# Stores of the gated values moved to GpSimd's queue, a half-tile wait, and another pass order for the third tile, in a two-layer decoder kernel

## The reference

```python
def swiglu(x, w_gate_up, w_down):
    gu = x @ w_gate_up
    g, u = jnp.split(gu, 2, axis=-1)
    return (jax.nn.silu(g) * u) @ w_down
```

## Time and profile before

| | |
|---|---|
| median of the runs | 1989.75 us (1989.35 to 1995.39, 3 runs) |
| profiled execution | 1989.12 us, its span 1987.1 us |
| granted clock of TensorE | 0.999 |
| TensorE busy | 1968.9 us, 99% of the span |
| VectorE busy | 1317.0 us, 66% |
| ScalarE busy | 921.7 us, 46% |
| GpSimd busy | 1208.8 us, 61% |
| DMA | 414.99 MB, mean 209 GB/s |

### The profile page before, as it was taken

One profiled execution on the slowest core, in us unless ns is written; L12 is line 12 of the kernel. 1 busy time (PEld: TensorE's weight loads), 2 busy tenths in 40 slices (PEclk: granted clock), 3 DMA queues, 4 the chain that ended last, 5 costly groups with the idle time before them and its releaser, 6 DMA issues.

```text
span 1987.1 us, 28787 instructions
## 1 busy us (share of the span) xinstructions
PE 1968.9 (99%) x9979; PEld 1654.7 (83%) x9979; DVE 1317.0 (66%) x1749; ACT 921.7 (46%) x1930; POOL 1208.8 (61%) x1055
## 2 busy tenths in 40 slices
PE   9999999999999999999999999999999999999998
PEld 8898988888888888888888788788888888887886
DVE  6765452688777877564675677779766676645567
ACT  7434333366544555432345465456554544432233
POOL 5343222657988898656664112474988888846566
PEclk9999999999999999999999999999999999999999
DMA  7574545835767878795853123553667667687683
GB/s 219 181 238 170 172 158 210 309 119 170 257 229 261 255 242 255 245 402 168 273 181 75 43 93 100 187 184 121 226 219 250 230 222 258 210 340 264 220 266 129
DMA packets 292628, 414.99 MB, mean 209 GB/s; under 512 B 38129, under 2 KB 215305, under 8 KB 292497
## 3 DMA queue, kind: packets, MB, share of 16 engines
q1 hardware_dynamic: 257792, 307.61, 47.3%
q10 hardware_dynamic: 33280, 100.94, 14.0%
q0 software_dynamic: 1424, 4.77, 0.7%
HBM read 259.09 MB, written 154.17 MB: 208 GB/s over the span
## 4 chain that ended last, share of the span: by engine, by line
PE 95%; DMA 2%; DVE 1%; ACT 1%; issue 0%; POOL 0%; SPq 0%; POOLq 0%; DVEq 0%; ACTq 0%
PE ps L2552 22%; PE ps L2554 22%; PE ps L2553 22%; PE ps L2463 9%; PE ps L2465 5%; DMA scratch_hidden<-hidden 1%; PE ps L2928 1%; PE ps L2772 1%; PE ps L2773 1%; PE ps L2769 1%; PE ps L2607 1%; PE ps L2902 1%; PE ps L2571 1%; PE ps L2573 1%; PE ps L2572 1%; PE ps L2813 1%
## 5 line engine op out<-in xcount | busy, mean ns | idle before, releaser
L2552 PE MATMUL ps<-forms,mats 128*128 128x512 f32 x2016 | 787.1, 390 | 4.4 <-DVE X L1893 3.0
L2554 PE MATMUL ps<-forms,mats 128*128 128x512 f32 x2016 | 784.6, 389 | 0.0
L2553 PE MATMUL ps<-forms,mats 128*128 128x512 f32 x2016 | 784.5, 389 | 0.0
L1097 POOL TENSOR_TENSOR mats<-sum_a,mats 128x256 fp32r<-128x256 f32 (+2 forms) x384 | 407.3, 1066 | 347.5 <-ACT mats L1349 346.6
L2552 PEld LDWEIGHTS ps<-forms,mats 128*128 128x128 f32 x2016 | 378.5, 188 | 86.1 <-issue 7.6
L2554 PEld LDWEIGHTS ps<-forms,mats 128*128 128x128 f32 x2016 | 378.5, 188 | 78.6
L2553 PEld LDWEIGHTS ps<-forms,mats 128*128 128x128 f32 x2016 | 378.6, 188 | 77.2
L1893 DVE TENSOR_TENSOR X<-ps,X 128x512 f32<-128x512 f32 x390 | 268.0, 690 | 191.6 <-PE ps L2554 186.1
L1349 ACT ACTIVATE mats<-sum_a 128x256 fp32r<-128x256 f32 (+2 forms) x392 | 201.3, 516 | 316.8 <-PE ps L2554 295.7
L1870 DVE TENSOR_TENSOR mats<-stream_raw,mats 128x256 fp32r<-128x256 f32 (+2 forms) x302 | 279.9, 929 | 21.3 <-ACT mats L1349 20.8
L1349 ACT ACTIVATE mats<-stream_raw 128x256 fp32r<-128x256 f32 (+2 forms) x302 | 156.4, 519 | 241.1 <-PE ps L2554 241.0
(11 more groups left out here) (271 smaller groups left out, 2621.1 us busy)
## 6 DMA issues: line engine op xcount, KB each, us to landing
forms<-scratch_forms ACTq DMA_DIRECT2D x182, 512.0 KB, 5.7
scratch_forms<-prep_forms SPq DMA_DIRECT2D x161, 512.0 KB, 3.3
stream_raw<-in_w_gate_up_dram SPq DMA_DIRECT2D x88, 512.0 KB, 5.5
scratch_forms<-head_forms SPq DMA_DIRECT2D x49, 512.0 KB, 3.2
scratch_hidden<-hidden SPq DMA_DIRECT2D x84, 256.0 KB, 5.3
prep_raw<-in_w_down_dram SPq DMA_DIRECT2D x38, 512.0 KB, 5.2
stream_raw<-scratch_hidden SPq DMA_DIRECT2D x32, 512.0 KB, 4.8
forms<-scratch_forms SPq DMA_DIRECT2D x28, 512.0 KB, 6.0
```

Of the source, the lines that this page charges most:

```text
L1097: pool.tensor_tensor(blocks(m[:, q, 1, :], it.width), stream_source(it, q), blocks(m[:, q, 0, :].bitcast(F32), it.width), ALU.subtract).th ...
L2552: mm(dst, ah, bh, start=OPENS[q] and k == 0, stop=False, skip_group_check=True)
L2553: mm(dst, ah, bl, start=False, stop=False, skip_group_check=True)
L2554: m = mm(dst, al, bh, start=False, stop=k == w - 1, skip_group_check=True)
```

## The change

Three parts.

First, the third tile (t = 2) of the value and gate stage is no longer `v_gate_tile(2)`, which takes the three passes interleaved for each of eight blocks k. Its high-by-high and high-by-low passes come first, for all k, waiting for ScalarE's high parts and the PSUM bank that is written; the low-by-high pass follows and waits for VectorE.

Second, in the plain item product j = 2 waits for the first half of the last tile's evacuation alone.

Third, `store_hidden` moves from SyncE's queue to GpSimd's. SyncE had issued the 22 pairs of a layer at i = 9, then between its other transfers at q = 1 and q = 3 of i = 10 to 27, and at 28, 29 and 31. GpSimd issues all 22 pairs, at q = 1 of i = 9 to 30, each for the item before. Its waits for `u_dve` (that VectorE has written the tile) and the transfers themselves are unchanged.

```diff
@@ SyncE @@
-            def store_hidden(it, halves=range(2)):
-                l, k = it.layer, up_no[it.n]
-                for e in halves:
-                    sp.wait_ge(u_dve, 5 * k + 4 + e)
-                    sp.dma_start(scr_h[l][:, :, it.tile, e, :].rearrange("g p n -> p g n"),
-                                 hidden_of(it)[e][:].rearrange("p (g n) -> p g n", g=4)).then_inc(hid_st[e], 16)
...
-                    if i in (9, 28, 29):
-                        store_hidden(its[i - 1])
-                    if i == 31:
-                        store_hidden(its[29])
...
                             if 10 <= i <= 27 and q in (0, 2):
                                 load_stream(its[i + 2], (q // 2,))
-                            if 10 <= i <= 27 and q in (1, 3):
-                                store_hidden(its[i - 1], (q // 2,))
@@ GpSimd @@
+            def store_hidden(it):
+                l, k = it.layer, up_no[it.n]
+                for e in range(2):
+                    pool.wait_ge(u_dve, 5 * k + 4 + e)
+                    pool.dma_start(scr_h[l][:, :, it.tile, e, :].rearrange("g p n -> p g n"),
+                                   hidden_of(it)[e][:].rearrange("p (g n) -> p g n", g=4)).then_inc(hid_st[e], 16)
...
                     for q in range(NQ):
+                        if 9 <= i <= 30 and q == 1:
+                            store_hidden(its[i - 1])
@@ TensorE, plain_item @@
                     if j == 2:
-                        pe.wait_ge(xt_ready, evac_before[norm] + 16)
+                        pe.wait_ge(xt_ready, evac_before[norm] + 15)
@@ TensorE, value and gate stage @@
-            for t in range(2, TT):
+            pe.wait_ge(xt_hi_ready, 6)
+            pe.wait_ge(bank_free[6], Kv[0][6])
+            for k in range(KT):
+                v_gate_pass(2, "hh", (k,), first=True)
+                v_gate_pass(2, "hl", (k,))
+            pe.wait_ge(bank_free[0], Kn[0] + 2)
+            pe.wait_ge(bank_free[1], Kn[1] + 2)
+            v_gate_pass(2, "lh", range(KT), last=True)
+            x_transposes(0, Kn, 4)
+            for t in range(3, TT):
```

## The result

The changed kernel takes 2039.93 us (median of 5 runs, 2036.45 to 2041.51) against 1989.35 us for the kernel before (5 runs): ratio 1.0249, 95% interval 1.0235 to 1.0263. It is slower by 50 us. The prediction was 1991.4 with a range of 1985 to 2003. The profiled execution has a span of 2037.9 us against 1987.1.

The account below looks back on a forecast made before the run. TensorE was taken as the bound, so time is won only where it stands still. Gains 4.3 us, losses 5.9, net +1.6 on the profiled 1989.12 gave 1990.7, or 1991.4 as the runs' median; range 1985 to 2003.

Parts of the forecast that it names:

- The cost of GpSimd's load: Up stages: 36 stores per window at 0.7 us each fit GpSimd's spare time; 0.6 us lost in all.
- The overloaded GpSimd: Every up-stage item: from 1.15 us per store GpSimd sets the pace, about 2013 to 2070 us; chance 0.14.
- The rival in which one of the two engines starves the other: Up stages: VectorE's two-input operations lengthen GpSimd's issue to 1.2 us per store, 1993 to 1999 us; chance 0.04.
- The first store: Start of up stages: later first stores delay prep loads 5.8 us; TensorE stops 2.2 us per layer at item 10's fifth product.
- The end of the stage: End of up stages: earlier last stores gain 2.7 us at X tile 0 but cost 0.9 in the activation forms' loads.
- The gain: Near 884 and 1800: X tile 0 loads sooner, so TensorE's stops for the residual addition go; 2.7 us.
- The forms' loads: End of up stages: activation-form loads slowed by stores beside them, 0.7 us in layer 1, 0.2 in layer 0.
- the 0.3 taken: Third tile, 20.48: the reorder removes a 0.58 us TensorE stop, of which 0.3 us is taken as gain.
- the slack at the gates: Gate transposes at 45.59: their input is ready 0.15 us earlier, limiting the third tile's gain to between 0.15 and 0.58.
- its named lower end of 0: Half-tile wait, 437.49 and layer 1: 1.28 us gain taken, but 0 if the next x form is as late.

Follow-up runs that it names:

- The memset run: Kernel before with parts 1 and 2, stores on SyncE, plus two GpSimd memsets of 128 x 512 at the changed kernel's store places: 1987.39 us, ratio 1.0004.
- the run with parts 1 and 2 alone: Kernel before with the third-tile reorder and half-tile wait only, stores left on SyncE: 1988.2 us, ratio 0.9994.
- with small DMAs: Kernel before with parts 1 and 2, stores on SyncE, plus two 4 KB GpSimd DMAs at the changed kernel's store places: 2055.44 us, ratio 1.0339.

## Why the prediction was wrong

**The cost of GpSimd's load: the step that failed.** The size of an issue was right, 0.7 against 0.76. The step after it was wrong: "while GpSimd issues, VectorE's operation is short and the next sum may be 0.44 shorter". Both halves are true, and together they hide the price. The operation is short only if it is through well before GpSimd reads again. If not, GpSimd's sums are indeed shorter, 1.3 instead of 1.74 us, because VectorE is held for two to six of them. The saved time of GpSimd is the lost time of VectorE, and TensorE waits behind VectorE. The term stood in the sum with 0.6 us (ends 0 and 3). TensorE falls 28.7 us behind in layer 0's up stage and 22.7 in layer 1's, half clock included. The memset run shows that the rows alone could not give it away: without an issue, the same overlap costs nothing.

**The rivals.** The overloaded GpSimd gave the right side but not the mechanism. It asked for 1.15 us per store; the issue took 0.76, and GpSimd was busy for 85% of the up stage, less than before. The rival in which one of the two engines starves the other had them reversed: it let VectorE lengthen the issue (1.2 us, it stayed at 0.76), while the issue lengthened VectorE. The Trainium skill, page "SBUF — State Buffer", section "Who interferes with whom", has tensor_tensor in conflict with GpSimd's reads alone, and takes GpSimd's descriptor writing to leave it alone, as an inference. The measured 4.70 us of an instruction begun in an issue, and its return to 0.68 with a pause behind it, decide against reading that as harmless.

**The clock.** No term stood for it. In the changed kernel the nine stops of 2.2 us or more are each followed by work at half clock, until 3.0 to 5.3 us behind the stop; the three of 1.4 to 1.9 us are not. No exact bound follows: with one memset behind the stores a stop of 2.0 us was followed by half clock, and with the stores at the fifth product one of 3.0, at 484, was not. With 15.3 us this is nearly a third of the loss. A forecast of many stops of 4 us would have had to add it.

**The first store.** Predicted 2.2 us per layer; there is no stop near 484. The place and the order were right, but the stores landed after 2.9 us, not 5.2 (from ScalarE's queue, 11 us earlier, 2.3 to 2.8; from SyncE's before the change 6.6 to 7.0). The prep loads went out at 471.47, 3.0 us later than before instead of 5.8, and the prep sum took 1.29 us instead of 1.74. So the term was mis-sized, below its lower end of 0.6.

**The end of the stage.** The gain came: the residual addition's wait fell from 3.0 to 0.6 us, and TensorE makes up 0.8 us there in layer 0 and 2.0 in layer 1, 2.8 where 2.7 was taken. The forms' loads lost more than the 0.7 taken: the load that TensorE waits for in layer 1 landed after 10.3 us, not 8.8, and the stop became 2.68 us from 1.23, plus its half clock.

**Parts 1 and 2.** At the third tile TensorE gains 0.67 us. In the changed kernel it reached the tile 0.47 us earlier than before for a reason that lies ahead of the changed code, and then waits for the gates, which take 0.28 back: 0.39 is left, near the 0.3 taken. In the run with parts 1 and 2 alone it came only 0.06 earlier and 0.6 is left. So the slack at the gates was a real bound, and how much it takes depends on the start of the execution. Part 2 gave 0.73 and paid it back 20 us later, its named lower end of 0, though for a low part of the weights and not for an x form.

## What to carry to other kernels

A DMA issued by GpSimd costs more than GpSimd's time: look for VectorE instructions with two inputs in SBUF that will run beside it, and for what waits behind them. Here the same stores were free from SyncE's or ScalarE's queue. If GpSimd must issue, let it next do something that does not read SBUF for about as long as VectorE's instruction takes (0.53 us was enough for the time here, 0.13 was not); it costs GpSimd's time. And if a change makes stops of 3 us or more, add the slow clock behind most of them.

## What the runs showed of the hardware

- A VectorE tensor_tensor of 128 x 512 with both inputs in SBUF, begun during GpSimd's issue of a DMA and not through when GpSimd begins to read again, was held for up to 7.2 us (11 of 12 such in the changed kernel were over 1.9 us). Of 20 that should have been through in time 8 were lengthened, to between 1.3 and 4.1 us. With one input in PSUM all 15 begun in an issue took 0.69 at most.
- The instruction need not begin in the issue: with small DMAs one that began 2.4 us behind it, in a row of GpSimd's reading instructions, took 8.18 us.
- The issue takes GpSimd 0.533 us for one piece, 0.549 for 128 pieces of 32 bytes, 0.760 for 512 pieces of 512 bytes. SyncE took 0.454 for the last, ScalarE's queue 0.482.
- Behind the issue a pause of 0.13 us did nothing; pauses of 0.53 and of 1.13 us both saved 39 us of 50. With 0.53 us 17 of 23 two-input instructions were still lengthened, most to 1.3 to 1.8 us; with 1.13 none was.
- What makes GpSimd, behind an issue, not let VectorE in for several instructions, while it does so behind a memset, stays open; no run here looks inside.
